# Ten transformer sublayers with streamed weights: turned tiles in three parts in other banks, the first tile's layer-norm statistics on VectorE, and sums, loads and waits placed elsewhere

## The reference, cut to what matters

```python
    for l in range(DEPTH):                                  # first_block
        h = rmsnorm(x, g_mix_pre[l])
        ...
        x = x + rmsnorm(mix, g_mix_post[l])
        xo = cross_attention(rmsnorm(x, g_x_pre[l]), rmsnorm(mem, g_x_mem[l]), w_xq[l], w_xkv[l], w_xo[l])
        x = x + rmsnorm(xo, g_x_post[l])
        gate, up = jnp.split(rmsnorm(x, g_ffn_pre[l]) @ w_ffn_in[l], 2, axis=-1)
        f = (jax.nn.silu(gate) * up) @ w_ffn_out[l]
        x = x + rmsnorm(f, g_ffn_post[l])
    for i in range(DEPTH):                                  # second_block
        m = (s_c @ ada_w[i] + ada_b[i]).reshape(B, N_MOD, 1, D)
        x = half_step_ffn(x, m[:, 0], m[:, 1], m[:, 2], ffn_w_in[i, 0], ffn_w_out[i, 0], ln_g[i, 0], ln_b[i, 0])
        ...
        x = post_norm_update(x, y_lat, m[:, 5], 1.0, ln_g[i, 1], ln_b[i, 1])   # layer_norm(ALPHA * x + gate * y)
```

## Time and profile before

| | |
|---|---|
| runs | 2231.2, 2234.15, 2239.68 us, median 2234.15 |
| profiled execution | 2223.64 us, span 2221.8 us, granted clock 0.994 |
| busy | PE 2141.1 (96%), POOL 1684.8 (76%), ACT 1069.0 (48%), DVE 968.2 (44%) |
| HBM | 444.60 MB read, 201 GB/s |

### The profile page before, as it was taken

The page is one execution under the profiler, slowest core; times in us unless marked ns, Lnnn a source line. Parts: engine busy times, 40 slices in busy tenths (PEclk is TensorE's granted clock), DMA queues, the critical chain, the costliest instruction groups (busy, mean ns, idle before and its releaser), DMA issues.

```text
span 2221.8 us, 32201 instructions
## 1 busy us (share of the span) xinstructions
PE 2141.1 (96%) x10197; PEld 1735.5 (78%) x10197; DVE 968.2 (44%) x1892; ACT 1069.0 (48%) x1646; POOL 1684.8 (76%) x1361
## 2 busy tenths in 40 slices
PE   9998999989998999999999989999999999999997
PEld 7787788777876887788778867887887788787886
DVE  7456676744557453444545442354112210434112
ACT  5555444345544544544544354565444444445442
POOL 6546498876463988888898878727988888797986
PEclk9999999999999999999999999999999999999999
DMA  7536487854354877687787865524666566464663
GB/s 256 165 106 207 137 282 244 286 168 149 106 180 156 279 256 268 232 278 256 283 294 255 313 189 160 163 73 138 199 188 196 165 184 215 139 217 149 195 205 119
DMA packets 135863, 447.10 MB, mean 201 GB/s; under 512 B 22539, under 2 KB 28131, under 8 KB 135769
## 3 DMA queue, kind: packets, MB, share of 16 engines
q1 hardware_dynamic: 130232, 427.24, 58.6%
q10 hardware_dynamic: 5536, 18.61, 2.4%
HBM read 444.60 MB, written 3.03 MB: 201 GB/s over the span
## 4 chain that ended last, share of the span: by engine, by line
POOL 49%; issue 27%; PE 21%; DVE 2%; POOLq 1%; DMA 0%; ACT 0%; SPq 0%; ACTq 0%; DVEq 0%
POOL w_lo L815 48%; PE ps L2159 6%; PE ps L2161 6%; PE ps L2160 6%; PE ps L2671 1%; PE ps L2636 1%; PE ps L2659 1%; PE ps L2499 1%; POOLq L191 0%; PE ps L2632 0%; POOL ada_land L861 0%; POOLq L813 0%; PE ps L2602 0%; PE ps L2414 0%; DMA cols<-cols_dram 0%
## 5 line engine op out<-in xcount | busy, mean ns | idle before, releaser
L815 POOL TENSOR_TENSOR w_lo<-land,w_hi 128x512 fp32r<-128x512 f32 x1300 | 1648.4, 1300 | 489.4 <-ACT w_hi L920 488.0
L920 ACT ACTIVATE w_hi<-land 128x1024 fp32r<-128x1024 f32 x654 | 692.7, 1061 | 927.7 <-PE ps L2161 714.5
L2159 PE MATMUL ps<-w_hi,h_hi 128*128 128x512 f32 (+1 forms) x1840 | 731.4, 398 | 44.6 <-DVE h_lo L1504 22.0
L2161 PE MATMUL ps<-w_hi,h_lo 128*128 128x512 f32 (+1 forms) x1840 | 718.7, 391 | 0.0
L2160 PE MATMUL ps<-w_lo,h_hi 128*128 128x512 f32 (+1 forms) x1840 | 717.7, 390 | 0.0
L2159 PEld LDWEIGHTS ps<-w_hi,h_hi 128*128 128x128 f32 x1840 | 346.7, 188 | 136.9 <-issue 43.9
L2161 PEld LDWEIGHTS ps<-w_hi,h_lo 128*128 128x128 f32 x1840 | 346.5, 188 | 73.7
L2160 PEld LDWEIGHTS ps<-w_lo,h_hi 128*128 128x128 f32 x1840 | 347.2, 189 | 67.2
L1546 DVE TENSOR_TENSOR hid_lo<-ps,hid_hi 128x512 f32 (+1 forms) x77 | 53.2, 691 | 550.9 <-ACT hid_hi L1060 550.9
L2159 PE MATMUL ps<-w_hi,hid_hi 128*128 128x512 f32 x616 | 245.1, 398 | 1.1 <-POOL w_lo L815 1.0
L2160 PE MATMUL ps<-w_lo,hid_hi 128*128 128x512 f32 x616 | 243.5, 395 | 0.0
(11 more groups left out here) (276 smaller groups left out, 1907.5 us busy)
## 6 DMA issues: line engine op xcount, KB each, us to landing
land<-ffn_w_in_dram SPq DMA_DIRECT2D x220, 512.0 KB, 3.6
ada_land<-ada_w_dram SPq DMA_DIRECT2D x144, 512.0 KB, 5.4
land<-ffn_w_out_dram SPq DMA_DIRECT2D x110, 512.0 KB, 3.7
land<-w_ffn_in_dram SPq DMA_DIRECT2D x88, 512.0 KB, 4.0
land<-w_ffn_out_dram SPq DMA_DIRECT2D x44, 512.0 KB, 4.2
land<-na_w_qkv_dram SPq DMA_DIRECT2D x40, 512.0 KB, 4.1
land<-w_xkv_dram SPq DMA_DIRECT2D x32, 512.0 KB, 3.7
land<-w_in_dram SPq DMA_DIRECT2D x32, 488.0 KB, 3.5
```

Source lines behind the costliest of these rows:

```text
L815: done = pool.tensor_tensor(w_lo[:, slot, half], land[:, slot, half], w_hi[:, slot, half].bitcast(F32), ALU.subtract)
L920: act.activation(w_hi[:, slot, :], land[:, slot, :], ACT.Copy).then_inc(*my.up("hi_ready"))
L2159: pe.matmul(dst, lh, wh, start=first, stop=False)
L2161: done = pe.matmul(dst, ll, wh, start=False, stop=last)
```

## The change

- Turned tiles of `rms` and `ln` come in three parts (two, two and four transposes) in banks 4, 6 and 5 instead of two halves; DVE's and ACT's orders of `affine`, `high`, `low`, `square_y` and `scale_y` change with it. Holding matmuls write bank 1, one instead of two before tile 0 is turned.
- `ln` takes the first tile's mean and variance on DVE in halves (`half_of_first`, `bn_stats`), without ACT's `variance(0)` and shift.
- The product `ffn_w_in_200` (context rows) starts aside.
- The first group of `products_na` goes by pairs of units (`BY_PAIRS`).
- The bias tables are loaded between units of the product before neighbourhood attention (`na_w_kv`), not all after its fourth unit.
- One adaptive group moves from `products_y` of layer 1's cross attention to the feed-forward output of layer 1, step 17; layer 0's sum at step 17 moves to step 18; the columns are read at step 14, not 9, and SP stores a group at step 11.
- In cross attention `ada_sum` stands after the first two scores, `copy_turned` before the first exponentials.

```diff
-ADA_OUTS, ADA_OUTS_2, ADA_OUTS_3, COLUMNS_AT = (8, 13, 17), (8, 13), (8, 12, 16), 9
+ADA_OUTS, ADA_OUTS_2, ADA_OUTS_3, COLUMNS_AT = (8, 13, FC - 4), (8, 13, 17), (8, 12, 16), 14
-HELD = (2, 2, 1)
+HELD = (1, 2, 1)
+BY_PAIRS = ((0, (0, 1)), (1, (0, 1)), (0, (2, 3)), (1, (2, 3)))
+        def piece(parts, i):
+
+            t, p = divmod(i, parts)
+            if parts == 2:
+                return t, 4 * p, 4, TURN + i
+            return (t, *((0, 2, TURN), (2, 2, OUT), (4, 4, TURN + 1))[p])
...
-                do("products_y", f"w_xo{l}", ada_load=True, sums=1 + l)
+                do("products_y", f"w_xo{l}", ada_load=True, sums=1)
...
-            do("ffn_in", "ffn_w_in_200", ada=True)
+            do("ffn_in", "ffn_w_in_200", ada=True, aside=True)
...
             def products(w, groups, width, dst, then=None, aside=False):
-                first = 8 if w == "na_w_kv" else 0
-                stream("na_w_qkv" if w == "na_w_kv" else w, first, 4 * groups)
+                assert w == "na_w_kv"
+                extra = {RING + 2 * h: lambda h=h: load_bias(h) for h in range(NA_BIAS)}
+                extra[RING - 1] = load_tables
+                stream("na_w_qkv", 8, 4 * groups, extra, rolled=False)
...
-                extra = ada_extra([at - 3 for at in ada])
+                extra = ada_extra([min(at - 3, FC - 8) for at in ada])
                 if columns is not None:
-                    extra[3] = lambda: stored[0] < group[0] and stored[0] < ADA_GROUPS and ada_store()
-                    extra[5] = lambda had=extra.get(5): (ada_rows(columns), had and had())
+                    extra[3] = lambda: stored[0] < group[0] and ada_store()
+                    extra[11] = lambda had=extra.get(11): (had and had(), stored[0] < ADA_GROUPS and ada_store())
+                    extra[13] = lambda had=extra.get(13): (ada_rows(columns), had and had())
...
                 act.wait_ge(sems["w_used"], my.at("w_used", n["w_used"]))
...
+                _, high = halves("x", gain, parts=3)
+                high(0)
+                split(1)
+                high(1)
                 if not early:
                     square_y(1, 0)
                 square_y(1, 1)
-                if gain is None:
-                    split(1)
-                    return
-                _, high = halves("x", gain)
-                high(0)
-                high(1)
-                split(1)
-                high(2)
-                high(3)
+                for i in range(2, 6):
+                    high(i)
...
-                split(1)
-                variance(0)
-                split(2)
+                split(3)
                 normalise(0)
                 split(1)
...
-                affine, high = halves("z", folded=folded)
+                affine, high = halves("z", folded=folded, parts=3)
+                affine(1)
                 high(0)
-                affine(1)
                 high(1)
+                affine(2)
+                high(2)
+                variance(1)
                 normalise(1)
...
+                        if m == 0:
+                            copy_turned(2, TURN)
+                            copy_turned(3, TURN + 1)
                         if m < len(maps):
                             exps(m)
-                        if m == 0:
-                            copy_turned(2, TURN)
-                            copy_turned(3, TURN + 1)
...
                 affine(0)
                 affine(1)
                 low(0)
+                affine(2)
+                low(1)
                 if not early:
                     scale_y(1, 0)
                 step(scale_y(1, 1))
-                low(1)
+                low(2)
                 new_x(1)
...
+                def half_of_first(half):
+
+                    b = bank(half)
+                    step(scale_y(0, half))
+                    step(dve.scalar_tensor_tensor(b, tile[:, 0, half * GW:(half + 1) * GW], ALPHA, b, ALU.mult, ALU.add))
+                    step(dve.bn_stats(moments[:, half, :], b))
...
-                affine, low = halves("z", folded=folded)
+                affine, low = halves("z", folded=folded, parts=3)
                 affine(0)
-                low(0)
+                add_x(1)
+                for i in range(3):
+                    low(i)
                 deviation(1)
...
+                    if (j, half) == (1, 1) and FC - 4 in ada:
+                        ada_sum()
...
                     score(0)
                     score(1)
+                    ada_sum()
                     pe.wait_ge(sems["taken"], my.at("taken", n["taken"]))
-                    turn_free()
-                    for kp in (2, 3):
-                        turn_query(kp, TURN + kp % 2)
+                    turn_free(but=("ada_sum",))
+                    turn_query(2, TURN)
+                    pe.wait_ge(sems["ada_sum"], my.at("ada_sum", n["ada_sum"]))
+                    turn_query(3, TURN + 1)
```

More of the change, by code:

```diff
@@ L703, in products_y @@
                     return
[L704 to L707, removed]
+                extra = ada_extra([3 if keys else 0])
                 if keys:
@@ L1114, in rstd_x, with halves @@
                 n["rstd"] += 1
-            def halves(src, gain=None, mod=None, folded=None):
+            def halves(src, gain=None, mod=None, folded=None, parts=2):
                 if gain is None and n["mcol"] == 0:
@@ L1120, in halves @@
                 v0, a0 = n["turned_v"], n["affine"]
-                n["turned_v"] += 4
-                n["affine"] += 4 if gain is not None else 2
-                n["split_lo"] += 4
+                n["turned_v"] += T * parts
+                n["affine"] += T * parts if gain is not None else T
+                n["split_lo"] += T * parts
                 mine = {}
@@ L1128, in affine @@
                     act.wait_ge(sems["turned_v"], my.at("turned_v", v0 + i + 1))
-                    for k in range(4):
-                        scale, shift = affine_columns(4 * (i % 2) + k, 1, mod, folded)
-                        at = turned_bank(i)[:, k, :]
+                    _, first, count, _ = piece(parts, i)
+                    for k in range(count):
+                        scale, shift = affine_columns(first + k, 1, mod, folded)
+                        at = turned(parts, i)[:, k, :]
                         done = act.activation(at, at, ACT.Identity, scale=scale, bias=shift)
@@ L1194, in rms @@
                 act.wait_ge(sems["w_used"], my.at("w_used", n["w_used"]))
+                if gain is None:
+                    if not early:
+                        square_y(1, 0)
+                    square_y(1, 1)
+                    split(1)
+                    return
+                _, high = halves("x", gain, parts=3)
+                high(0)
+                split(1)
+                high(1)
                 if not early:
@@ L1715, in new_x @@
                                              ALU.mult, ALU.add).then_inc(*my.up("x_new"))
-                affine, low = halves("x", gain) if gain is not None else (lambda i: None, lambda i: None)
+                affine, low = halves("x", gain, parts=3) if gain is not None else (lambda i: None, lambda i: None)
                 scale_y(0, 0)
@@ L1728, in rms @@
                 step(scale_y(1, 1))
-                low(1)
+                low(2)
                 new_x(1)
-                for i in (2, 3):
-                    affine(i)
-                for i in (2, 3):
-                    low(i)
+                affine(3)
+                affine(4)
+                low(3)
+                affine(5)
+                low(4)
+                low(5)
             def ln(src, res, units, early=False, folded=None):
@@ L2128, in _ @@
             later = []
+            in_parts = [2]
             def start():
@@ L2183, in group, with group_by_tile @@
                         after[j]()
-            def group_by_tile(banks, width, fresh=False, after=None, left=(h_hi, h_lo)):
+            def group_by_tile(banks, width, fresh=False, after=None, left=(h_hi, h_lo), pairs=False):
                 u = n["units"]
@@ L2387, in products_y @@
                     o0, p0 = n["o_taken"] - X_H, n["probs"] - X_H
[L2388 to L2391 removed]
+                    group((0, 2), GW, True, after={0: lambda: turn_head_x(KC // 2 - 1, o0, p0)})
                 else:
@@ L2525, in ready @@
                         pe.wait_ge(sems["x_new"], my.next("x_new", want - n["x_new"]))
+                parts = 2 if now else 3
                 def turn_tile(t):
                     ready(t)
-                    for k in range(KC):
-                        done = pe.transpose(turned_bank(2 * t + k // 4)[:, k % 4, :], TILES[src][:, t, k * P:(k + 1) * P], ident[:, :])
-                        if k % 4 == 3:
-                            done.then_inc(*my.up("turned_v"))
+                    for i in range(parts * t, parts * (t + 1)):
+                        _, first, count, _ = piece(parts, i)
+                        for k in range(count):
```

(7 more changed lines are left out.)

101 lines of the change are left out of this document (49 added, 52 removed).

## The result

The changed kernel takes 2215.47 us (median of 10 runs, 2209.55 to 2222.48) beside 2229.64 for the kernel before (10 runs): the medians differ by 14.2 us, and the ratio is put at 0.9934 with a 95% interval of 0.9916 to 0.9952, which is 14.7 us less (10.7 to 18.7). Three of the runs of before had been shown ahead, with a median of 2234.15, and that is why the stated time of 2220 us lies 4.5 above the measured one while the difference fits: on the ratio the forecast of -13.8 stands for 0.9938.

What follows compares the result with a forecast made beforehand. PE was taken as the bound, busy 2141.1 of 2221.8 us. The terms sum to -13.8 us, taking the profiled 2223.64 to 2209.8, and the ratio 1.0047 gives a median of 2220 us, range 2207 to 2230.

Steps and rivals of the forecast that it cites:

- Bias loads: Kv product before neighbourhood attention: spreading SP's run of 24 loads shortens PE's 7.42 us wait; -7.5 us (-4 to -8.6).
- the other aside group: Group behind a layer norm at 1116.52: first weights come sooner, the norm being about 0.5 us shorter; -0.5 us.
- Group out of `products_y`: Layer 1 cross attention: moving the adaptive sum out removes waits of 1.28 and 2.66 us and slow clock; -5.1 us.
- into `ffn_out`: Layer 1 feed-forward output, step 17: the moved sum brings waits of about 0.4, 1.8 and 0.9 us; +3.1 us.
- `rms` joints: Five joints: tile 1 starts sooner, but POOL, not PE, sets the next group; +2.6 us (-7 to +5).
- Rival A: `rms` and `ln` joints gain in full, tile 1's earlier start being kept; sum -28.1, 2206 us; chance 0.13.
- `ln` joints: Four joints: the first gives 0.9, the last 0.33, the second takes 0.9; -1.3 us (-6 to +2).
- `BY_PAIRS`: Start of `products_na`: PE's idle time becomes one piece of about 3.6 us, half a chance of slow clock; +0.8 us.
- Rival B: PE's waits at joints or behind masks bring half clock, six at about 1.6 us; sum -4.2, 2230 us; chance 0.13.
- Rival C: Spread bias loads make weight units late through the kv product, 2.1 us each for 12; 2245 us; chance 0.04.
- Rival D: New sum in `ffn_out` as bad as the old, +5 and a 1.6 dip; 2224 us; within the main case's 0.70.
- The signs of being wrong: PE's waits for `h_lo` (22.0) fall over 8 us without POOL's growing, or clock dips behind a wait under 2 us.

Runs made afterwards that it cites:

- experiment 7: Kernel before with the bias loads spread and nothing else; 2224.44 us, ratio 0.9980.
- Experiment 11: Changed kernel with ACT's variance of the first tile back at all layer-norm joints, one run; four folded joints give -2.1 us instead of -5.7.
- experiment 8: Changed kernel with the adaptive group back in `products_y` of layer 1, out of step 17; 2214.29 us, ratio 0.9924.
- experiment 5: Kernel before with ACT's squares of x made early inside the `rms` joints; 2226.98 us, ratio 0.9990.
- experiments 2: Changed kernel with ACT's squares of x made early inside the `rms` joints; 2210.28 us, ratio 0.9910.
- 6: Changed kernel with two halves instead of three parts at the `rms` joints alone; 2212.34 us, ratio 0.9926.
- experiment 10: Changed kernel with two holding matmuls again before tile 0 is turned at layer-norm joints, one run; four folded joints give -4.2 us instead of -5.7.
- Experiment 9: Changed kernel with early squares and one weight unit ahead, first group of `products_na` by tiles again; 2201.03 us, ratio 0.9878.
- experiment 4: Changed kernel with early squares of x and one weight unit rounded ahead at layer norms without folded columns; 2201.62 us, ratio 0.9870.
- experiments 1: Changed kernel again with no edit, giving its second profiled execution; 2212.64 us, ratio 0.9921.
- 3: Changed kernel with one weight unit rounded ahead at layer-norm joints without folded columns; 2206.81 us, ratio 0.9896.

## Why the prediction was right

The median moved by 14.2 us of an expected 13.8, but not every term was as good as their sum. By place the changed stretches gave 10.2 and 14.0 us.

- *Bias loads:* -7.5 (the terms as written add up to 7.37) against -5.3. The mechanism was right, and experiment 7 shows it alone, with 1.36 + 0.38 + 0.45 left where I had 1.26 (before the half microsecond off) and 0.5. What failed is the step "since the layer norm ends sooner", here and for the other aside group (-0.5, measured +0.7). The norm of tile 0 ends later there, and the wait that was to be under 1.5 us is 2.31. DVE is busy with the turned rows of the new product before and then has six operations of 0.7 us, where it had two of 0.7 and one of 1.4 and ACT's squares came after. Experiment 11 puts it at 0.9.
- *First context group:* -2.9 against -3.1 and -3.2. Right.
- *Group out of `products_y`* -5.1 against -7.0, and *into `ffn_out`* +3.1 against +4.0 and +5.3. The waits in `ffn_out` were right to half a microsecond (0.56, 1.42, 1.07 for 0.4, 1.8, 0.9, a sum of 3.05). Mis-sized is the step "the matmuls of the sum itself are only moved", which I counted on neither side: 2 x 0.23 = 0.5 belongs in both. In the first execution another 1.3 is the slow clock at the transposes, which in the second did not come. At the old place the 0.69 us that PE waits for x stand in the row of the joints, so it gave 6.3 where I had 5.1, and 0.7 of that stays unexplained. The net, -2.0, was predicted, and -1.7 and -3.0 measured; experiment 8 has about 1. The kernel before lost 1.6 us at the old place to a slower clock, which experiments 5 and 8 did not lose there and experiment 7 did. So the gain of moving this group is small, and most of it depends on whether the clock falls.
- *Layer 0's sum:* -2.5 against -2.8. Right. *Cross attention:* -0.5 against 0.0 and -0.8, within what two executions differ by. The mechanism is not shown: in layer 1 the wait for `qT_x` went from 1.81 to 1.28 and 1.03, but layer 0 has one of 1.43 and 0.94 where it had 0.34.
- *`rms` joints:* the step "a tie: POOL, not PE, sets the next group" was right, shown by experiments 2 and 5 together and by 6 from the other side. The cost came out at +4.0 (3.3 without that 0.69) for +2.6. Three joints cost what had been said: 0.35 and 0.39 for 0.4, and 0.98 for 1.0. The other two cost 0.7 and 0.9 for 0.4, and there PE waits 0.56 and 0.55 us for DVE's x before tile 1's turn, a wait that before didn't have and that the sum left out. Rival A, which kept the joints' gain, falls.
- *`ln` joints:* the step that failed is "the second takes 0.9". z of tile 1 is late by 1.10, as said, but I left the old wait behind that turn (0.98) standing, when the smaller pieces remove it; and the first tile gives 1.3, not 0.9. Each joint gives 1.2 to 1.7 for 0.3. Of the 5.7, experiment 11 gives the statistics 3.6 and experiment 10 the hold 1.4. The two overlap, since a shorter hold helps only where z is early, so they don't leave a clean rest for the pieces.
- *`BY_PAIRS`:* PE's 1.17 became 3.38, as predicted (3.6), and +0.8 was half the chance of a slower clock, 1.6. The clock fell behind this wait in all nine traces with pairs, and in none of the four by tiles. The place costs 3.5 and 2.0, of which 2.9 and 1.4 lie from 1352 on, where the pairs are. Experiment 9 bears it out in its trace, though the medians don't resolve it.
- *Rival B* is right in places (901, 1370) and wrong as a whole: most waits of the joints got shorter. *Rival C* did not come: 0.40 and 0.47 at two units, where it needed 2.1 at each of 12. *Rival D* came halfway: the waits in `ffn_out` are those of the main line, but the clock fell behind them in four traces of nine.
- *The signs of being wrong:* one of the two appeared. `h_lo` fell by 15.9 us, and POOL's wait grew, as it had to. But the clock did fall behind waits under 2 us: 1.42 and 1.07 at 901, 1.51 at 1449. What failed is the step from one full-speed stretch behind 1.80 to "short ones don't": the last section counts how often they do.

The largest errors point opposite ways: 4.3 us more gained than said at `ln` and 1.9 at `products_y`, against 2.2 less at the bias loads, 1.2 to 2.7 more lost at `products_na`, 0.9 to 2.2 at `ffn_out`, 1.4 at the `rms` joints and 1.2 at the other aside group. That the sum fits to within 1 us is largely luck.

Both edits together (experiment 4) make a version that beats both kernels: 2201.62 us, 0.9870 of the kernel before.

## What to carry to other kernels

When one engine's wait is shortened at a joint, look for the engine that ends within a few tenths of it: here POOL ended 0.06 us from PE, and took back all that the pieces gave until ACT's squares were moved into its idle time. An in-order engine that waits for a statistic is a place for work that the next stage needs; one weight unit there, at two places, was worth 5.9 us, as much as the bias loads alone (6.1) or the four folded joints (5.7). And a change of 0.6% that is made of ten parts is read place by place in two traces; the spans of two executions differed here by 1 us where the medians differed by 14.

## What had not been expected

**The start has two courses.** Up to 41 us no kernel here differs in code, and yet the traces fall into two groups 4 to 5 us apart: before and experiments 2, 9 and 10 early, the changed kernel and experiments 1, 3 to 8 and 11 late. DVE and POOL before:

```profile
20.07 0.18 DVE L1443 TENSOR_SCALAR ang<-ang 128x32 f32<-128x32 f32 x1
20.29 0.18 DVE L1444 TENSOR_SCALAR ang<-ang 128x32 f32<-128x32 f32 x1
20.50 2.67 DVE L1446 SCALAR_TENSOR_TENSOR ang<-ang 128x32 f32<-128x32 f32 x3
...
20.58 16.43 POOL L815 TENSOR_TENSOR w_lo<-land,w_hi 128x512 fp32r<-128x512 f32 x13 [19.60 <-ACT w_hi L920]
```

and in the changed kernel:

```profile
21.44 1.22 DVE L1454 TENSOR_SCALAR ang<-ang 128x32 f32<-128x32 f32 x1
22.69 1.22 DVE L1455 TENSOR_SCALAR ang<-ang 128x32 f32<-128x32 f32 x1
...
20.07 12.64 POOL L818 TENSOR_TENSOR w_lo<-land,w_hi 128x512 fp32r<-128x512 f32 x10 [19.09 <-ACT w_hi L923]
```

The same small operation on SBUF takes 0.18 us before POOL begins its stream and 1.22 after, which is near the length of one POOL operation (1.27). POOL began 0.5 us sooner (20.07) and DVE came to these steps 0.4 later, so four more of them fell under it, and PE waited 3.2 us for what they lead to. What counts is the distance of the two: from DVE's `pos_r`, a little ahead of these steps, to POOL's first `w_lo` it is 0.70 to 0.76 us in the nine late traces and 1.58 to 1.79 in the four early ones. The Trainium skill (SBUF — State Buffer, "SBUF: two separate sides") says that VectorE and GpSimd share one port pair, which a GpSimd operation, and a VectorE operation in a two-port mode or with two inputs in SBUF, locks for the whole instruction; the trace agrees, with 1.22 beside 1.27, though no run here tells which VectorE operations are concerned and why. So a shift of under 1 us between two engines made the kernel 4 to 5 us later.

What decides between the two courses I did not try to find, but it isn't the change: the kernel before was early and experiments 5 and 7, which edit it elsewhere, were late; the changed kernel was late twice and experiment 10, which differs from it in one constant, early. The early traces are among the faster executions of their kernels (2223.64 for a median of 2229.64, 2204.20 for 2210.28), so probably each execution falls into one or the other; that is not shown.

**The clock falls behind some short waits and not behind others.** The same code with the same wait gives both. In the mixer's attention PE waits 1.6 us (1.62 at 604.66 in the changed kernel), in all thirteen traces, and the clock fell to its lower level in it or right behind it in seven. Behind the 1.5 in the neighbourhood attention it fell in six of thirteen, behind 1.42 and 1.07 in `ffn_out` in four of nine, and behind the 3.4 at the start of `products_na` in nine of nine. Behind 1.80 at the joints it fell at two of five in experiment 5 and nowhere in before. No run here tells what decides behind the short ones. A fall costs mostly 1.3 to 1.6 us, and about 3 at two places of the first execution of the changed kernel, and that is most of what two executions of one kernel differ by: 6.7 us between the two spans of the changed kernel, of which 1.4, 1.3, 1.5 and 1.6 are at 604, 901, 1370 and 1449.
